# A mixture-of-experts router that forms its slot lists with matrix products instead of a scatter through DRAM

## What is computed

```python
def hier_moe(h, w_grp, w_exp, w1, w3, w2):          # h: 512 tokens x 1024
    grp_prob = softmax(xt @ w_grp)                   # 4 groups
    p_g, g_sel = top_k(grp_prob, 1)
    sel_logits = (xt @ w_exp).reshape(T, 4, 8)[group g_sel]
    top_l, top_e = top_k(sel_logits, 2)              # two experts of that group
    gate = softmax(top_l) * p_g
    ...                                              # sort the 1024 choices by expert, blocks of 128
    y = (silu(xb @ w1[e]) * (xb @ w3[e])) @ w2[e]    # 32 experts, 1024 -> 512 -> 1024
    out = segment_sum(y * gate, token)

x = x + hier_moe(rmsnorm_2(x, g_ffn), ...)
x = x + sigmoid(rmsnorm_2(x, g_ple) @ w_pg) * (p @ w_ple)
```

## Time and profile before

| | |
|---|---|
| median of 3 runs | 2122.65 us (2118.94 to 2126.57) |
| the profiled execution | 2117.9 us, its span 2115.9 us |
| TensorE, VectorE, ScalarE, GpSimd busy | 86%, 39%, 24%, 2% of the span |
| DMA traffic | 353.72 MB, mean 167 GB/s |
| DMA issues of expert weights | 96 of 2048 KB, median 28 us from issue to landing |

### The profile page before, as it was taken

The page is one execution under the profiler, slowest core; times in us unless marked ns, Lnnn a source line. Parts: engine busy times, 40 slices in busy tenths (PEclk is TensorE's granted clock), DMA queues, the critical chain, the costliest instruction groups (busy, mean ns, idle before and its releaser), DMA issues. The chain is left out here.

```text
span 2115.9 us, 20762 instructions
## 1 busy us (share of the span) xinstructions
PE 1821.9 (86%) x8299; PEld 1298.3 (61%) x8299; DVE 826.8 (39%) x1357; ACT 510.4 (24%) x872; POOL 35.4 (2%) x55
## 2 busy tenths in 40 slices
PE   6899789989987999999699559988689888898865
PEld 6787677766676888788588446656434334344344
DVE  1662488742144222233622463224213223223343
ACT  2312066631124222232333222113100000000032
POOL 0000000000000000000000000000100000000000
PEclk9899589999998999999799879999689999999988
DMA  8565000023251332313123101135369999999921
GB/s 319 182 250 170 21 1 1 1 98 102 80 159 40 104 96 83 117 60 120 50 81 98 40 0 60 60 153 208 111 281 427 427 427 427 426 427 427 424 91 40
DMA packets 100764, 353.72 MB, mean 167 GB/s; under 512 B 8974, under 2 KB 62906, under 8 KB 84922
## 3 DMA queue, kind: packets, MB, share of 16 engines
q1 hardware_dynamic: 98106, 343.98, 42.2%
q0 software_dynamic: 2560, 8.40, 1.0%
HBM read 343.93 MB, written 6.33 MB: 166 GB/s over the span
## 5 line engine op out<-in xcount | busy, mean ns | idle before, releaser
L537 PE MATMUL up_ps<-up_h,up_w 128*128 128x512 f32 x352 | 137.8, 391 | 5.7 <-DVE up_h L532 5.7
L538 PE MATMUL up_ps<-up_h,up_w 128*128 128x512 f32 x352 | 137.5, 391 | 0.0
L539 PE MATMUL up_ps<-up_h,up_w 128*128 128x512 f32 x352 | 137.4, 390 | 0.0
L2064 PE MATMUL ex_h<-s_ab,u_big_tail 128*64 128x512 f32 x400 | 122.6, 635 | 12.8 <-DMA s_ab<-in_w 6.1
L2064 PE MATMUL ex_h<-ring,u_big_tail 128*64 128x512 f32 x512 | 114.9, 596 | 11.6 <-DMA ring<-in_w 11.1
L514 PE MATMUL merge_ps<-s_ab,ring 128*128 128x512 f32 x256 | 114.4, 594 | 4.7 <-PE merge_ps L514 2.7
L537 PE MATMUL merge_ps<-merge_h,merge_w 128*128 128x512 f32 x256 | 105.9, 414 | 0.7 <-DVE merge_h L532 0.7
L532 DVE TENSOR_TENSOR p_w<-ring,p_w 128x1024 fp32r<-128x1024 f32 x44 | 53.9, 1226 | 134.4 <-ACT p_w L577 134.4
L532 DVE TENSOR_TENSOR merge_w<-ring,merge_w 128x1024 fp32r<-128x1024 f32 x32 | 39.2, 1226 | 156.1 <-ACT merge_w L577 156.1
L539 PE MATMUL merge_ps<-merge_h,merge_w 128*128 128x512 f32 x256 | 99.9, 390 | 0.0
L538 PE MATMUL merge_ps<-merge_h,merge_w 128*128 128x512 f32 x256 | 99.6, 389 | 0.0
(11 more groups left out here) (446 smaller groups left out, 3707.7 us busy)
## 6 DMA issues: line engine op xcount, KB each, us to landing
ring<-in_w SPq DMA_DIRECT2D x48, 2048.0 KB, 28.4
s_ab<-in_w SPq DMA_DIRECT2D x36, 2048.0 KB, 27.6
reg_a<-in_w SPq DMA_DIRECT2D x12, 2048.0 KB, 32.2
ring<-in_w_in SPq DMA_DIRECT2D x11, 2048.0 KB, 7.9
ring<-in_w_ada SPq DMA_DIRECT2D x16, 1024.0 KB, 4.9
ring<-in_w_in SPq DMA_DIRECT2D x16, 1024.0 KB, 7.2
ring<-in_w_ffn_gate SPq DMA_DIRECT2D x11, 1024.0 KB, 5.4
ring<-in_w_ffn_up SPq DMA_DIRECT2D x11, 1024.0 KB, 8.0
```

The lines of the kernel that those rows point to most:

```text
L537: nc.tensor.matmul(ps, x[0], y[0], start=start, stop=False)
L538: nc.tensor.matmul(ps, x[0], y[1], start=False, stop=False)
L539: return nc.tensor.matmul(ps, x[1], y[0], start=False, stop=stop)
L2064: mm = nc.tensor.matmul(ps[half, :], xT[:, k, half], ws[j][:, k, cols], start=(k == 0), stop=(k == k_end - 1))
```

## The change

The choice of experts stays as it is; what changes is how the logits reach VectorE, how the lists of tokens are made, and where the spill part and half of the embedding products are done.

- **Logits.** `b.wr` is padded with zeros to 64 columns per feature tile (a memset on GpSimd ahead of its two loads). TensorE now holds the weights and streams the tokens: 8 products of 512 columns into two halves of a bank. VectorE copies the sums, and 4 products with `join` (two unit matrices above one another) turn them and add the halves.
- **Ranks.** 5 products with 160, 128, 96, 64 and 32 columns take the place of 14 with 32.
- **Lists.** `by_rank` holds for every choice a 1 at its rank (64 columns), `values` its token number or weight at its expert. 16 products of 32 columns make the lists of the 32 experts' 64 slots in `ps_t`, in place of the scatter, the read back and the turn.
- **Spill.** The slot numbers that go with spill blocks (`spill_slots`) are now made by VectorE at the start of the expert stage, ahead of `x_in(0)`. GpSimd scatters the pairs to DRAM after the gather of pair 1, SyncE reads the list back ahead of matrix 24, and it is turned inside `stage_spill`, only if there is a spill block.
- **Embedding products.** Pieces 0 to 3 stay in the router, spread between its steps; pieces 4 to 7 run at the start of the expert stage ahead of `turn(0)`. Matrix 6 is loaded after the eighth, so from the expert stage. The loads of `p` and `w_ple` go ahead of the zeroing of `tok_list` in SyncE's list.

```diff
+        b.wr = b.scr[:, U:2 * U].rearrange("p (k n) -> p k n", k=KD)
...
+                sp.wait_ge(b.wr_clear, 1)
...
+                nc.gpsimd.memset(b.wr, 0.0).then_inc(b.wr_clear, 1)
...
+def early_product(nc, b, pe, ps, i):
+
+    return product_rows(nc, ps[:], b.pT, i // 2, b.ple_w[:, :, i % 2 * CH:(i % 2 + 1) * CH], 2)
+
+
+def keep_product(nc, b, ps, i):
+
+    return nc.scalar.copy(b.pw[:, i // 2, i % 2 * CH:(i % 2 + 1) * CH], ps[:])
...
-            sp.wait_ge(pool, 7)
-            sp.dma_start(b.tok_dram.rearrange("(b s) o -> b (s o)", s=P), zeros[0:SLOTS // P, :]).then_inc(zero, 16)
             sp.wait_ge(b.rows_saved, 16)
             sp.dma_start(prow, a["p_2"][0, 0].rearrange("(t p) n -> p t n", p=P)).then_inc(p_in, 16)
-            sp.dma_start(ple, feature_tiles(a["w_ple_2"][0], 0, D)).then_inc(p_in, 16)
+            sp.dma_start(b.ple_w, feature_tiles(a["w_ple_2"][0], 0, D)).then_inc(p_in, 16)
+            sp.wait_ge(pool, 8)
+            sp.dma_start(b.tok_dram.rearrange("(b s) o -> b (s o)", s=P), zeros[0:SLOTS // P, :]).then_inc(zero, 16)
             sp.wait_ge(logits, 1)
             load_expert(b, sp, 7)
-            sp.wait_ge(ple_done, 2 * NT)
-            load_expert(b, sp, 6)
-            sp.wait_ge(scat, 16 * 2 * NT)
-            sp.dma_start(toks[0:SLOTS // P, :], b.tok_dram.rearrange("(b s) o -> b (s o)", s=P)).then_inc(back, 16)
+            sp.wait_ge(zero, 16)
...
-            g.wait_ge(slots_, 1)
-            g.wait_ge(zero, 16)
-            for i in range(2 * NT):
-                nc.gpsimd.indirect_dma_start(b.tok_dram, bass.IndirectOffsetOnAxis(b.slot[:, i:i + 1], 0),
-                                             entry[:, i, :], None).then_inc(scat, 16)
...
         def _(pe):
             pe.wait_ge(b.wr_in, 32)
-            for t in range(NT):
-                mm = product_rows(nc, ps_l[:, t * NE:(t + 1) * NE], b.hT, t, b.wr, KD)
+            for k in range(KD):
+                half = slice(64 * (k % 2), 64 * (k % 2) + 64)
+                mm = nc.tensor.matmul(ps_l[half, :], b.wr[:, k, :], b.hT[:, k, :], start=(k < 2), stop=(k >= KD - 2))
             mm.then_inc(logits, 1)
...
+            pe.wait_ge(joined, 1)
+            pe.wait_ge(lg_out, 1)
+            for t in range(NT):
+                mm = nc.tensor.matmul(ps_lt[:, t * NE:(t + 1) * NE], lgT[:, t * P:t * P + P], join, start=True, stop=True)
+            mm.then_inc(turned_in, 1)
             pe.wait_ge(p_moved, 2)
+            for i in range(2):
+                early_product(nc, b, pe, ps_p[i], i).then_inc(b.ple_done, 1)
+            pe.wait_ge(pool, 8)
+            pe.wait_ge(masks, 1)
+            nc.tensor.matmul(ps_r[:, 0:(NT + 1) * EXPERTS], before, both.rearrange("p t e -> p (t e)"),
+                             start=True, stop=False, skip_group_check=True)
+            for d in range(1, NT + 1):
+                mm = nc.tensor.matmul(ps_r[:, d * EXPERTS:(NT + 1) * EXPERTS], b.ones[:],
+                                      both[:, 0:NT + 1 - d, :].rearrange("p t e -> p (t e)"),
+                                      start=False, stop=(d == NT), skip_group_check=True)
+            mm.then_inc(ranks, 1)
+            early_product(nc, b, pe, ps_p[2], 2).then_inc(b.ple_done, 1)
+            pe.wait_ge(placed, 3)
             for i in range(2 * NT):
-                if i >= 4:
-                    pe.wait_ge(ple_out, i - 3)
-                product_rows(nc, ps_p[i % 4][:], pT, i // 2, ple[:, :, i % 2 * CH:(i % 2 + 1) * CH], 2).then_inc(ple_done, 1)
-            pe.wait_ge(pool, 7)
-            pe.wait_ge(masks, 1)
...
-            pe.wait_ge(back, 16)
-            for i in range(2):
-                at_ = i * (SLOTS // P)
-                mm = nc.tensor.transpose(ps_t[:, at_:at_ + SLOTS // P], toks[0:SLOTS // P, i::2], b.ident[0:SLOTS // P, 0:SLOTS // P])
-            mm.then_inc(turned, 1)
+                for j in range(2):
+                    mm = nc.tensor.matmul(ps_t[64 * j:64 * j + 64, 0:2 * PAIRS], by_rank[:, i, :],
+                                          values[:, i, j].rearrange("p v s -> p (v s)"), start=(i == 0), stop=(i == 2 * NT - 1))
+            mm.then_inc(lists, 1)
+            early_product(nc, b, pe, ps_p[3], 3).then_inc(b.ple_done, 1)
 
         @block.scalar
         def _(act):
             for k in range(2):
                 act.wait_ge(p_turned, k + 1)
-                nc.scalar.copy(pT[:, k, :], ps_p[k][:]).then_inc(p_moved, 1)
-            for i in range(2 * NT):
-                if i == 3:
-                    act.wait_ge(expin, 1)
-                    nc.scalar.activation(eg, eg, ACT.Exp).then_inc(expd, 1)
-                act.wait_ge(ple_done, i + 1)
-                nc.scalar.copy(b.pw[:, i // 2, i % 2 * CH:(i % 2 + 1) * CH], ps_p[i % 4][:]).then_inc(ple_out, 1)
+                nc.scalar.copy(b.pT[:, k, :], ps_p[k][:]).then_inc(p_moved, 1)
+            act.wait_ge(expin, 1)
+            nc.scalar.activation(eg, eg, ACT.Exp).then_inc(expd, 1)
             act.wait_ge(expin, 2)
             nc.scalar.activation(e2, e2, ACT.Exp).then_inc(expd, 1)
+            for i in range(4):
+                act.wait_ge(b.ple_done, i + 1)
+                keep_product(nc, b, ps_p[i], i).then_inc(b.ple_out, 1)
...
+            nc.vector.tensor_tensor(join, b.ident[:, 0:NE], b.ident[:, 64:64 + NE], ALU.add).then_inc(joined, 1)
             dve.wait_ge(logits, 1)
-            link(nc.vector.tensor_copy(lg, ps_l[:, 0:NT * NE].rearrange("p (t n) -> p t n", t=NT)))
+            nc.vector.tensor_copy(lgT, ps_l[:]).then_inc(lg_out, 1)
+            dve.wait_ge(pool, 8)
+            dve.wait_ge(turned_in, 1)
+            link(nc.vector.tensor_copy(lg, ps_lt[:, 0:NT * NE].rearrange("p (t n) -> p t n", t=NT)))
...
+            nc.vector.tensor_tensor(both[:, 0:NT, :], oh1, oh2, ALU.add).then_inc(masks, 1)
             nc.vector.tensor_tensor(e2, m2, m1, ALU.subtract).then_inc(expin, 1)
+            paired = oh.rearrange("p i (s j) -> p i s j", j=2)
+
+            def spread(v, which):
+                return nc.vector.tensor_tensor(values[:, :, :, which, :].rearrange("p i j s -> p i s j"), paired,
+                                               v.unsqueeze(2).unsqueeze(3).to_broadcast([P, 2 * NT, PAIRS, 2]), ALU.mult)
+            spread(b.entry[:, :, 0], 0).then_inc(placed, 1)
...
+            spread(b.weight[:], 1).then_inc(placed, 1)
+            nc.vector.tensor_copy(b.entry[:, :, 1], b.weight[:])
...
+            link(nc.vector.tensor_copy(b.rank, ps_r[:, 0:(NT + 1) * EXPERTS].rearrange("p (t n) -> p t n", t=NT + 1)))
...
+                last = nc.vector.tensor_tensor(tt[:, k * NT:(k + 1) * NT, :], oh[:, k * NT:(k + 1) * NT, :], b.rank[:, 0:NT, :], ALU.mult)
+            link(last)
+            link(nc.vector.tensor_reduce(at_rank, tt, AX.X, ALU.add))
+            nc.vector.tensor_tensor(by_rank, wide(at_rank, CAP), io64.unsqueeze(1).to_broadcast([P, 2 * NT, CAP]),
+                                    ALU.is_equal).then_inc(placed, 1)
+            dve.wait_ge(lists, 1)
+            nc.vector.tensor_copy(b.tok[:, 0:PAIRS], ps_t[:, 0:PAIRS])
+            nc.vector.tensor_copy(b.tokf[:, 0:PAIRS], ps_t[:, 0:PAIRS])
+            nc.vector.tensor_copy(b.share[:, 0:PAIRS], ps_t[:, PAIRS:2 * PAIRS])
...
+def spill_slots(b, dve, link, slots_):
+
+    nc, X, Xi, A, B, over, rank = b.nc, b.X, b.Xi, b.A, b.B, b.over, b.rank[:, 0:NT, :]
+    cnt, cmp_ = b.rank[:, NT, :], b.hmT.rearrange("p f s -> p (f s)").rearrange("p (a e) -> p a e", a=SPILL)
+    link(nc.vector.tensor_scalar(X, cnt, float(CAP), None, ALU.is_gt))
+    for more in range(CAP + P, T, P):
+        link(nc.vector.scalar_tensor_tensor(out=X, in0=cnt, scalar=float(more), in1=X, op0=ALU.is_gt, op1=ALU.add))
+    link(nc.vector.tensor_tensor_scan(out=Xi, data0=X, data1=X, initial=0.0, op0=ALU.add, op1=ALU.bypass))
...
+    link(nc.vector.tensor_reduce(b.slotf, b.picks, AX.X, ALU.add))
+    nc.vector.tensor_copy(b.slot[:], b.slotf).then_inc(slots_, 1)
...
+        ps_early = [ps_h3, ps_c, ps_y[0], ps_y[1]]
...
+            sp.wait_ge(b.ple_done, 2 * NT)
+            load_expert(b, sp, 6)
             for m in range(len(b.wbuf), 6 * PAIRS):
+                if m == 3 * len(b.wbuf):
+                    sp.wait_ge(scat, 16 * 2 * NT)
+                    sp.dma_start(b.toks[0:SLOTS // P, :], b.tok_dram.rearrange("(b s) o -> b (s o)", s=P)).then_inc(b.list_back, 16)
...
+                if s == 1:
+                    pool.wait_ge(slots_, 1)
+                    for i in range(2 * NT):
+                        nc.gpsimd.indirect_dma_start(b.tok_dram, bass.IndirectOffsetOnAxis(b.slot[:, i:i + 1], 0),
+                                                     b.entry[:, i, :], None).then_inc(scat, 16)
...
+            for i in range(4, 2 * NT):
+                early_product(nc, b, pe, ps_early[i - 4], i).then_inc(b.ple_done, 1)
             turn(0)
...
+                    if s == 0:
+                        pe.wait_ge(b.ple_out, 2 * NT)
...
```

(9 more changed lines are left out.)

158 lines of the change are left out of this document (80 added, 78 removed).

## The result

| | before | after |
|---|---|---|
| median of 5 runs, us | 2123.97 (2118.94 to 2126.57) | 2091.29 (2087.45 to 2094.19) |
| ratio, 95% interval | | 0.9849 (0.9836 to 0.9862) |
| profiled execution, us (its span) | 2117.9 (2115.9) | 2091.29 (2089.5) |

The change makes the kernel faster by 32.7 us of the medians. The forecast was 2098.5, with a range from 2090 to 2108. Between the spans of the two profiled executions the gain is 26.4.

A forecast was written before the change was run, and what follows sets the result against it. The expert stage's weight stream bounds the kernel: its start plus an unchanged 444.7 us. Starting at 1528.7 instead of 1552.91 gains 24.2, less 0.2 for added transfers: 2122.65 - 24.0, about 2098.5 us, range 2090 to 2108.

The forecast's parts named there:

- signs of being right: Trace checks: stream's first loads and last weight wait some 24 earlier, no 13 us wait for `e2`, lists in 2 to 6.
- Logits: Router: 16 records take 3.5 at full clock; `w_ple`, landing at 1488.8, sets the limit; VectorE starts at 1492.3, gain 0.8.
- Choice: Router, VectorE: chain to `e2` unchanged at 5.98, a new spread of 256 elements at 0.42, all done at 1500.5.
- Ranks: Router, TensorE: 480 columns in two passes, 1.6 at half clock or 0.8 at full, arriving at 1501.0.
- Lists: Router, TensorE: 32 records at 0.11 take 3.6, or 1.8 with paired halves; there at 1507.2.
- The expert stage's start: From router end at 1510.5 to first stream load at 1528.7: 18.2, between 16.8 and 19.5 by clock.
- What lies hidden: Expert stage's start: gather of pair 0 and `spill_slots` (6.4) fit under four embedding products (6.9) plus the turn.
- Added transfers: Stream's start: matrix 6 done before it, scatters mostly so, read back's wait long over; 0.2 us taken off the gain.
- Rival 1: TensorE stays at half clock through router and four products; stream starts at 1542.1, gain 11, 2111.7 us; chance 0.07.
- Rival 2: Gather of pair 0 waits for VectorE's `spill_slots`; 1 to 4 lost, gain 20 to 23, 2101 us; chance 0.06.
- Rival 3: No gain, because the stream's start does not set the kernel's end; 2122 us; chance 0.02.
- Rival 4: Scatters on GpSimd's queue hold up the gather of pair 2, drying the stream; 53 lost, 24 won, 2152 us; chance 0.03.

The follow-up runs named there:

- e6: The changed kernel with the turn of the joined logits ahead of the transposes of `p` in TensorE's list; 2085.22 us, ratio 0.9824 to the kernel before.
- e10: The changed kernel with three more groups of small products behind the lists, read by nothing; 0.035 a record in alternating halves, 0.070 in one half, 0.226 with 128 columns.
- e3: The changed kernel with embedding products 4 to 7 and the load of matrix 6 back in the router; 2102.49 us, ratio 0.9901 to the kernel before.
- e4: The changed kernel without the eight scatters of the spill lists, the read back no longer waiting for them; 2091.03 us, ratio 0.9854 to the kernel before.
- e1: The kernel before with both exponents ahead of ScalarE's eight copies of embedding products; 2122.98 us, ratio 1.0005.
- e2: The kernel before with the edit of e1 and the rank products ahead of the eight embedding products in TensorE's list; 2119.9 us, ratio 0.9989.
- e5: The kernel of e2 with the read back ahead of matrix 6 in SyncE's list; 2114.68 us, ratio 0.995 to the kernel before.

## Why the prediction was right

It named the place (the start of a stream that nothing else moves), the steps and their order, and these held. The time fell inside the range, 7.2 below the point and 1.3 from its fast end. That it did owes something to luck: the stream's start, the quantity that the prediction worked out, lies outside its own bounds. With 0.77 added they are 1525.1 to 1535.3 and it came at 1523.01, a gain of 30.7 for the 18.4 to 28.6 forecast. By the bounds of the stream alone the fast end would have been 2094.05 (2122.65 less 28.6), and only the 4 us that were added for the spread of the runs hold 2091.29 inside the range. Of the signs of being right, the lists' 32 records "in 2 to 6" failed too (1.13). The reading of the earlier trace rows was off by a slice: before, the DMA engines are full in slices 31 to 38, not from the 30th to the last but one; the sum does not use it. Step by step, from the first logits product (forecasts as on record, with 0.77 added):

| step | forecast | measured | off by |
|---|---|---|---|
| VectorE starts the choice | 1493.1 | 1492.36 | 0.7 |
| `e2` | 1499.1 | 1498.34 | 0.7 |
| ranks at VectorE | 1501.8 | 1500.39 | 1.4 |
| lists there | 1508.0 | 1503.65 | 4.3 |
| end of the router (ScalarE's last copy) | 1511.3 | 1506.14 | 5.1 |
| stream starts | 1529.5 | 1523.01 | 6.5 |

- **Logits.** 16 records took 3.65 for 3.5, and TensorE waited 2.93 for `w_ple`, the limit that the forecast named. e6 shows that the place of the turn behind this wait was the change's own weak point; it need not stand there. The prediction had seen the wait and not asked who is queued behind it without needing it.
- **Choice.** 5.98 again. The spread of 256 took 0.60, not 0.42: it is nearer to the row for 512 than I took it.
- **Ranks.** Forecast at half clock, 1.6; they ran at full clock (0.97 and 0.51 before it), which was back by 1495, during products 0 and 1. VectorE copied them as soon as its own list was done, without an idle stretch, so in the end that list and not the ranks set the time. This is 0.7 of the table.
- **Lists.** This is the step with the wrong size: 3.6 forecast, 1.13 measured, below even the lower bound of 1.8. The bound counted the paired halves and left the stationary side at 128 columns; e10 separates the two. With the 0.5 that I had given to waiting for embedding product 2, and that did not occur, it carries 2.9 of the 5.1 at the router's end. Another 0.8 is product 3 and its copy, 2.5 from the lists to the end for the forecast's 3.3.
- **The expert stage's start.** 18.2 forecast between the full clock's 16.8 and the half clock's 19.5; measured 16.87 (1506.14 to 1523.01). I stood between two levels, and the engine was on one of them throughout. That is 1.3.
- **What lies hidden.** The gather and `spill_slots` under the four products: no wait, as forecast. e3 puts a price on that cover, 11 us with matrix 6's collision in it, some 8 without (an estimate from e3's rows).
- **Added transfers.** 0.2 forecast; 0.9 between one trace with the scatters and one without (e4).
- **Rival 1** (half clock throughout): the clock is 1.00 from 1495 on. **Rival 2** (gather held up by VectorE): the gather took 1.11 beside VectorE for 0.98 alone, and nothing waited for it. The Trainium skill's rule of the shared port (SBUF — State Buffer, "SBUF: two separate sides"), carried through as a hold-up of the whole transfer, is not what this trace shows; whether any of these VectorE operations held that port, it doesn't tell. **Rival 3** fell with the last wait for weights moving 28.9. **Rival 4** (scatters hold up the gather of pair 2): it went out at 1526.21, and TensorE waited for no gather from there on.

e1, e2 and e5 speak to the part that the prediction did not have to price: what in the change brings the time. The reorder alone had looked like 9 to 11 us; it gave 2.3 until the read back was taken out from behind matrix 6. With e3 in between, the 33 us divide, to some 2 us, into three parts of 10 to 11: the order, the new lists with the wider logits and ranks, and the four products at the head of the expert stage.

## What to carry to other kernels

In a kernel that ends in one long stream of weights, look for what starts it, and price every step up to there by rows of the same shape; for a small product, columns of the stationary side and the half in which it lands each count by themselves. A 2 MB load issued 0.4 us ahead of a 32 KB one that everything waits for cost it 6.5 us, so when a chain becomes shorter, check which large transfer now falls into its place. Fill TensorE's waits with work that is needed later (11 us here, some 3 of them for a load that no longer meets the gather), and never let work that is needed now stand behind a load that it doesn't use (4.5 us here).

## What the runs showed of the hardware

- **The clock at its lower level while TensorE is busy.** In e10 TensorE was busy all the time from 1504 to 1511, and the granted clock averaged 0.51. Windows of e10:

```profile
1501.00:1504.00 3.00, 2.55 (x60) 2.55 (x60) 0.74 (x4) 0.30 (x1) 0.00 (x0) 1.00 0.00 0
1504.00:1511.00 7.00, 7.00 (x28) 5.11 (x26) 0.00 (x0) 0.00 (x0) 0.00 (x0) 0.51 0.00 0
1511.00:1516.00 5.00, 4.07 (x10) 1.79 (x10) 3.26 (x13) 1.17 (x2) 1.69 (x2) 1.00 0.22 50
```

  Before the clock fell, TensorE made 64 records of 32 columns (1501.45 to 1504.6). While it was down TensorE made 16 more of 32 columns and then, from 1508.02 on, embedding product 3 with 512 columns; from 1511 on the clock is 1.00 again. This is one execution.
- **A small read issued just behind a large load in the same queue:** 8.3 us from issue to reader with a 2 MB load 0.40 ahead of it, 1.8 with none (e2, e5).
- **Eight scatters of 8-byte entries**, issued from 1515.95 to 1524.93, around the stream's start at 1523.01: the stream is 0.9 in 445 longer than without them, one trace each (e4).
